# Gates of the recurrence on PSUM banks of their own, in regrouped blocks, with the engines' orders around them rewritten

## The reference

```
proj = h @ w_in[l]
xr, yr, q, k, v, g_a, g_b = jnp.split(proj, IN_SPLITS, axis=-1)
u  = causal_depthwise_conv(xr, conv_w[l], conv_b[l])        # width 4
r  = sigmoid(block_diag_linear(u, rg_w_a[l], rg_b_a[l]))    # 16 blocks of 88 x 88
i  = sigmoid(block_diag_linear(u, rg_w_x[l], rg_b_x[l]))
log_a = -8 * r * softplus(-lam);  a = exp(log_a)
inp = sqrt(-expm1(2 * log_a)) * (i * u)
hr = scan(h[t] = a[t] * h[t-1] + inp[t])
y_a = (gelu(yr) * hr) @ w_up_a[l]
```

## Time and profile before

| | |
|---|---|
| median of 3 runs | 2631.21 us (2628.38 to 2634.86) |
| profiled execution | 2633.96 us, span 2632.1 us |
| PE busy | 2610.1 us, 99% |
| POOL, ACT, DVE busy | 1127.0, 1116.0, 882.9 us |
| DMA | 263.01 MB, mean 100 GB/s |
| mean granted clock of TensorE | 0.997 |

### The profile page before, as it was taken

How to read it: one execution, slowest core, us unless ns; L and a number is a source line. 1 busy time by engine, 2 the same in 40 slices (tenths; PEclk the granted TensorE clock), 3 DMA queues, 4 the chain that set the end, 5 groups by cost and what they waited for, 6 DMA issues and landing times.

```text
span 2632.1 us, 31945 instructions
## 1 busy us (share of the span) xinstructions
PE 2610.1 (99%) x11808; PEld 2121.9 (81%) x11808; DVE 882.9 (34%) x1585; ACT 1116.0 (42%) x1635; POOL 1127.0 (43%) x478
## 2 busy tenths in 40 slices
PE   9999999999999999999999999999999999999999
PEld 7888887778877788888888888868788778888887
DVE  4223135661346332221132231447513453322210
ACT  5333245743546443332243332457435463433321
POOL 4444444355431344444444444444553314444443
PEclk9999999999999999999999999999999999999999
DMA  5333624323323223333333323343233232333322
GB/s 160 98 96 98 220 87 120 98 91 109 98 73 97 82 89 103 96 96 97 97 103 96 96 92 98 87 125 90 89 114 92 69 101 89 96 96 96 96 92 76
DMA packets 258134, 263.01 MB, mean 100 GB/s; under 512 B 9606, under 2 KB 242006, under 8 KB 258038
## 3 DMA queue, kind: packets, MB, share of 16 engines
q1 hardware_dynamic: 253542, 253.09, 32.3%
q10 hardware_dynamic: 4496, 8.58, 1.0%
HBM read 252.25 MB, written 10.57 MB: 100 GB/s over the span
## 4 chain that ended last, share of the span: by engine, by line
issue 47%; PE 30%; POOL 23%; POOLq 1%; DVE 0%
POOL wlo L551 23%; PE ps L1350 8%; PE ps L1355 8%; PE ps L1354 8%; PE ps L1563 1%; PE ps L1621 1%; PE ps L1636 1%; PE ps L1581 1%; PE ps L1586 1%; PE ps L1585 1%; POOLq L550 0%; POOLq L556 0%; PE ps L1543 0%; PE ps L1544 0%; PE ps L1413 0%
## 5 line engine op out<-in xcount | busy, mean ns | idle before, releaser
L551 POOL TENSOR_TENSOR wlo<-raw,whi 128x1024 fp32r<-128x1024 f32 x466 | 1125.7, 2418 | 1483.6 <-ACT whi L575 1483.5
L1350 PE MATMUL ps<-h_lo,whi 128*128 128x512 f32 x2272 | 890.0, 392 | 7.1 <-POOL wlo L551 6.2
L1354 PE MATMUL ps<-h_hi,whi 128*128 128x512 f32 x2272 | 887.0, 390 | 0.0
L1355 PE MATMUL ps<-h_hi,wlo 128*128 128x512 f32 x2272 | 886.6, 390 | 0.0
L575 ACT ACTIVATE whi<-raw 128x1024 fp32r<-128x1024 f32 x466 | 489.3, 1054 | 754.1 <-PE ps L1350 709.2
L1350 PEld LDWEIGHTS ps<-h_lo,whi 128*128 128x128 f32 x2272 | 428.3, 188 | 103.3 <-POOL wlo L551 7.9
L1355 PEld LDWEIGHTS ps<-h_hi,wlo 128*128 128x128 f32 x2272 | 428.1, 188 | 89.7
L1354 PEld LDWEIGHTS ps<-h_hi,whi 128*128 128x128 f32 x2272 | 428.3, 188 | 88.3
L1350 PE MATMUL ps<-act_lo,whi 128*128 128x512 f32 x704 | 274.1, 389 | 0.0
L1355 PE MATMUL ps<-act_hi,wlo 128*128 128x512 f32 x704 | 274.0, 389 | 0.0
L1354 PE MATMUL ps<-act_hi,whi 128*128 128x512 f32 x704 | 274.0, 389 | 0.0
(11 more groups left out here) (192 smaller groups left out, 2562.1 us busy)
## 6 DMA issues: line engine op xcount, KB each, us to landing
raw<-in_w_in SPq DMA_DIRECT2D x124, 512.0 KB
raw<-in_w_gate SPq DMA_DIRECT2D x88, 512.0 KB
raw<-in_w_up SPq DMA_DIRECT2D x88, 512.0 KB
raw<-in_w_down SPq DMA_DIRECT2D x80, 512.0 KB
rel_band<-rel_rows ACTq DMA_DIRECT2D x1, 8192.0 KB, 41.9
raw<-in_w_up_b SPq DMA_DIRECT2D x16, 512.0 KB
raw<-in_w_out SPq DMA_DIRECT2D x16, 512.0 KB
raw<-in_w_up_a SPq DMA_DIRECT2D x16, 384.0 KB
```

Source lines behind the costliest of these rows:

```text
L551: nc.gpsimd.tensor_tensor(wlo[:, s, :], raw[:, s, :], whi[:, s, :].bitcast(F32), ALU.subtract).then_inc(lo_made, 1)
L1350: ins = pe.matmul(ps[:, b, :], w_hi, x_lo, start=start, stop=False)
L1354: pe.matmul(ps[:, b, :], w_hi, x_hi, start=False, stop=False)
L1355: return pe.matmul(ps[:, b, :], w_lo, x_hi, start=False, stop=stop)
```

## The change

Gates get banks 6, 7, 0, 1 in turn, xr tiles 2 to 5; yr's banks are put in another order, the rest follows. Blocks are regrouped, the fifth group stands behind the first chunk of yr's first pair instead of behind the pair, and its order is 8, 14, 9, 15, 10. ACT does the sigmoids of a group ahead of the rounding of the next chunk; DVE does all of `u_gated` behind tile 10; the gelus are taken out of the loop that splits the product. SP's moves are put in between other loads.

```diff
--- before.py
+++ after.py
@@ -47,7 +47,7 @@
 
 NB = RNN // RB
 REST, MAIN = P - RB, KR
-GROUPS = [[0, 1], [2, 3, 11], [4, 5, 12], [6, 7, 13], [8, 9, 10, 14, 15]]
+GROUPS = [[0, 1], [2, 3], [4, 5, 11], [6, 7, 12, 13], [8, 14, 9, 15, 10]]
 GATED = [b for group in GROUPS for b in group]
 HELD = 4
 
@@ -334,17 +334,12 @@
         def mix_bank(n):
             return 2 + n % 6
 
-        def in_turn(*order):
-            bank, n = {}, 2
-            for kind, first, last in order:
-                for t in range(first, last):
-                    bank[kind, t] = mix_bank(n)
-                    n += 1
-            return bank
-
-        BANK = in_turn(("xr", 0, 6), ("gate", 0, 4), ("xr", 6, 8), ("gate", 4, 10), ("xr", 8, 10), ("gate", 10, 16),
-                       ("xr", 10, 11), ("gate", 16, 22), ("yr", 0, 2), ("gate", 22, 32), ("yr", 2, KR), ("g", 0, KD),
-                       ("ua", 0, KD), ("qk", 0, 2 * KD))
+        def laid(kind, *banks):
+            return {(kind, t): b for t, b in enumerate(banks)}
+
+        BANK = {**laid("xr", 2, 3, 4, 5, 2, 3, 4, 5, 2, 3, 4), **laid("gate", *[6, 7, 0, 1] * (NB // 2)),
+                **laid("yr", 5, 2, 7, 6, 3, 4, 5, 2, 7, 6, 3), **laid("g", 4, 5, 6, 7, 2, 3, 4, 5),
+                **laid("ua", 6, 7, 2, 3, 4, 5, 6, 7), **laid("qk", *[mix_bank(n) for n in range(2 * KD)])}
 
         V_BANKS = [4, 5, 2, 3, 6, 4, 5, 7]
         UB_T, OUT_T = 0, KD
@@ -454,29 +449,29 @@
                 pairs(w_in, KD, l, XR0 + 3 * PAIR, 1, G8)
                 gate_weights(1)
                 pairs(w_in, KD, l, XR0 + 4 * PAIR, 1, G8)
+                u_moves(l, 11)
                 gate_weights(2)
                 last_tile(XR0)
-                u_moves(l, 11)
                 gate_weights(3)
+                u_moves(l, 12)
                 half_pair(YR0, 0, 0)
-                u_moves(l, 12)
+                gate_weights(4)
                 half_pair(YR0, 0, 1)
-                gates_move(l, 11)
-                gate_weights(4)
                 u_moves(l, 13)
                 half_pair(YR0, 1, 0)
                 half_pair(YR0, 1, 1)
-                gates_move(l, 12)
+                gates_move(l, 11)
                 half_pair(YR0, 2, 0)
                 u_moves(l, 14)
                 half_pair(YR0, 2, 1)
+                u_moves(l, 15)
+                gates_move(l, 12)
                 gates_move(l, 13)
                 half_pair(YR0, 3, 0)
-                u_moves(l, 15)
+                gates_move(l, 14)
                 half_pair(YR0, 3, 1)
+                gates_move(l, 15)
                 half_pair(YR0, 4, 0)
-                gates_move(l, 14)
-                gates_move(l, 15)
                 half_pair(YR0, 4, 1)
                 last_tile(YR0)
                 pairs(w_in, KD, l, G0, KD // 2, G8)
@@ -754,30 +749,28 @@
                 act.wait_ge(decay_made, C.next(decay_made))
                 conv_init(6)
                 conv_init(7)
+                gates(2, 3)
                 ring()
-                gates(2, 3, 11)
                 conv_hi(6)
                 conv_hi(7)
                 ring(2)
                 conv_init(8)
                 conv_init(9)
+                gates(4, 5, 11)
                 ring()
-                gates(4, 5, 12)
                 conv_hi(8)
                 conv_hi(9)
-                ring(2)
+                ring()
                 conv_init(10)
                 gates(6, 7)
                 conv_hi(10)
-                gates(13)
+                gates(12, 13)
+                ring(2)
+                decayed(0, 2)
+                gates(8, 14, 9, 15, 10)
+                ring(2)
+                decayed(2, KR)
                 ring()
-                decayed(0, 2)
-                ring()
-                decayed(2, 4)
-                ring()
-                gates(8, 9, 10, 14, 15)
-                ring()
-                decayed(4, KR)
                 act.preload_act_table_set("natural_log_exp_and_others")
                 act.wait_ge(tanh_made, C.now(tanh_made))
                 for m in range(KR + 2):
@@ -796,19 +789,25 @@
 
 
 
-                ring()
-                for t in range(KR + 2):
-                    if t < KR:
+                def gelu(*tiles):
+                    for t in tiles:
                         b = BANK["yr", t]
                         C.step(bank_read[b])
                         act.wait_ge(bank_read[b], C.now(bank_read[b]))
                         nc.scalar.activation(y[:, t, :], y[:, t, :], ACT.Gelu_apprx_tanh
                                              ).then_inc(gelu_made, C.made(gelu_made))
-                    if t == KR:
+
+                ring()
+                gelu(0, 1, 2, 3)
+                ring()
+                gelu(4, 5, 6, 7)
+                ring()
+                gelu(8, 9, 10)
+                for t in range(KR):
+                    hi_of(ya_hi[:, t, :], tmp[:, t % 2, :])
+                    if t == 2:
                         act.preload_act_table_set("sigmoid_and_others")
-                    if t >= 2:
-                        hi_of(ya_hi[:, t - 2, :], tmp[:, t % 2, :])
-                    if t in (1, 3, 5, 7, 9, 11):
+                    if t in (1, 4, 7, 10):
                         ring()
 
                 for t in range(KD):
@@ -1129,6 +1128,7 @@
 
                 def u_gated(*tiles):
                     for t in tiles:
+                        dve.wait_ge(gate_made, gates_through(l, t))
                         for b in rest_of(t):
                             dve.wait_ge(gates_moved[(b - MAIN) % 2], moved(l, b, 2))
                         nc.vector.tensor_tensor(u[:, t, :], u[:, t, :], i_gate[:, t, :], ALU.mult
@@ -1139,12 +1139,10 @@
                 u_made(4, 5)
                 u_made(6, 7)
                 u_made(8, 9)
-                u_gated(0, 1)
                 u_made(10)
-                u_gated(2, 3)
+                u_gated(0, 1, 2, 3, 4, 5, 6, 7, 8, 9, 10)
                 yr_out(0)
                 yr_out(1)
-                u_gated(4, 5, 6, 7, 8, 9, 10)
 
                 for m in range(KR + 3):
                     if m in (3, 7, 11):
@@ -1485,8 +1483,8 @@
                 def xr(t, **how):
                     pair(G8, KD, (BANK["xr", t], BANK["xr", t + 1]), h_hi, h_lo, for_dve, t == 0, **how)
 
-                def yr(t):
-                    pair(G8, KD, (BANK["yr", t], BANK["yr", t + 1]), h_hi, h_lo, for_dve, False)
+                def yr(t, **how):
+                    pair(G8, KD, (BANK["yr", t], BANK["yr", t + 1]), h_hi, h_lo, for_dve, False, **how)
 
                 def gates(group):
                     s = chunk()
@@ -1521,8 +1519,7 @@
                 gates(GROUPS[2])
                 single(BANK["xr", KR - 1], h_hi, h_lo, for_dve)
                 gates(GROUPS[3])
-                yr(0)
-                gates(GROUPS[4])
+                yr(0, behind=lambda g: g == 0 and gates(GROUPS[4]))
                 yr(2)
                 yr(4)
                 yr(6)
@@ -1539,7 +1536,7 @@
                     for n in (t, t + 1):
                         C.step(square_made)
                         pe.wait_ge(square_split, C.next(square_split))
-                        pe.wait_ge(bank_read[n % 2], C.now(bank_read[n % 2]))
+                        bank_free(n % 2)
                         pe.matmul(ps[:, n % 2, :], ones_head[:, :], square_lo[:, n % 2, :], start=True, stop=False)
                         pe.matmul(ps[:, n % 2, :], ones_head[:, :], square_hi[:, n % 2, :], start=False, stop=True
                                   ).then_inc(square_used, C.made(square_used))
```

## The result

| | before | changed |
|---|---|---|
| median of 8 runs | 2632.69 us (2628.38 to 2635.36) | 2639.11 us (2637.64 to 2643.73) |
| profiled execution, span | 2633.96, 2632.1 us | 2641.95, 2640.2 us |
| mean granted clock | 0.997 | 0.993 |

The ratio is 1.003, 95% interval 1.0021 to 1.0039: slower by 6.4 us, or 8.1 us in the profiled executions. The forecast was 2616 us, 2603 to 2625; the kernel came out above that range.

The account below looks back on a forecast made before the run. The prediction took TensorE, busy 99% of the span, as the bound, with time lost only in late matmul starts. From 2631.2 us, -18.3 + 8.4 + 3.8 - 9.0 = -15.1 us gave 2616 us, range 2603 to 2625.

Parts of the forecast that it names:

- Most to gain: Late matmul starts from the first group's last gate to w_up_a, both layers: 27.6 us, 1.05% of the span.
- Banks: Gate groups up to yr: new banks remove PE's waits, 7.8 us in layer 0, 10.5 in layer 1, -18.3 us in total.
- with its own two turns of banks again 0.5 us in time: Gate group 4 (blocks 6, 7, 12, 13): its reused banks are free 0.5 us before PE needs them.
- Rival (b): New wait plus more: bank turns of groups 3 and 4 missed, or log phase not sooner; 2622 to 2628 us, 22%.
- New wait before block 15: Fifth gate group: PE waits for block 14's sigmoid, itself behind block 12's moves out; 4.2 us a layer, +8.4 us.
- The 2.0 us that the prediction quotes: Transfer setup and completion for the moves before block 15; with it the wait would be 3.3 us, the sum 1.8 better.
- The clock behind it: Matmuls after the wait before block 15 run at the low clock: 1.9 us each, +3.8 us, between 0 and 5.6.
- Later stretch: From yr to w_up_a: an earlier log phase and regrouped gelus remove PE's waits for wlo, -9.0 us.
- the moves are issued by 473.8 and landed at 476 to 477.3: Block 15's moves out, layer 0: so timed, they start the log phase near 481.6, 4.8 us sooner.
- Rival (c): Slower: block 12's moves land far later than 3.5 us after issue; at 12.5 us more per layer 2641 us; 4%.
- so no new wait: Before w_up_a: with the gelus out of it, the gated-product chain gets shorter, adding no wait.

Follow-up runs that it names:

- f2: f1 plus e4's edit (high halves of tiles 8 and 9 made ahead of the two roundings): 2607.49 us, ratio 0.9911.
- e4: Changed kernel, with ScalarE making the high halves of tiles 8 and 9 ahead of the two weight roundings, not between them: 2639.58 us, ratio 1.0026.
- f3: f2 with the gelus put back in the loop that splits the product: 2606.93 us, ratio 0.9903.
- e3: Changed kernel, with block 15's moves out put ahead of the load of chunk 23 on SyncE's list: 2630.03 us, ratio 0.999.
- e5: Kernel before, with the load of chunk 25 put ahead of block 15's moves out: 2638.72 us, ratio 1.0028.
- e2: Changed kernel, with g's banks reordered so that g tile 2 follows yr tile 7, not yr tile 9: 2632.86 us, ratio 1.0002.
- e1: Changed kernel, with block 12's moves out put ahead of the load of chunk 21 and block 15's input: 2631.48 us, ratio 0.9997.
- f1: Changed kernel, with the moves out of blocks 11, 12, 13, 15 and block 15's input each ahead of the load they stood behind: 2616.46 us, ratio 0.9942.
- e8: Changed kernel, with block 15's moves out put behind the load of chunk 24 as well as chunk 23: 2645.55 us, ratio 1.0047.
- e7: Changed kernel, with ScalarE again rounding the next chunk ahead of the sigmoids of groups 2 and 3: 2636.47 us, ratio 1.0016.

## Why the prediction was wrong, step by step

**Most to gain, 27.6 us: right.** f2 took 25.9 of it out of the two stretches.

**Banks, -18.3 us: the mechanism right, a margin wrong.** xr pair 6 and groups 2 and 3 start without a wait, and 39.97 us for the stage is what e4, f2 and f3 measured (40.06 forecast). It came to -11.9 us. The step that failed is "group 4 ..., with its own two turns of banks again 0.5 us in time": it took DVE's scaling of tile 10 as free to run, and left out that the sigmoids moved ahead push two roundings together (438.21 and 440.19), so that GpSimd subtracts twice without a break and DVE's splits last until just behind it. That cost 1.7 us of late start a layer, and 0.9 and 2.3 us of half-speed matmuls behind it within the stage. Rival (b) had named this, and the phase that isn't sooner, without a cause.

**New wait before block 15, +8.4 us: right in place and in chain, in size by luck.** It measured 3.7 + 4.6 = 8.3 us, but PE itself came some 3 us late to block 15, held by block 12's wait. e4 has the group stage that the forecast assumed (PE done with block 9 at 457.95, forecast 458.1), and there the same chain starts block 15 late by 7.2 and 7.4 us, 14.6 in all: block 13's sigmoid waits 1.8 us for block 11's moves, which the chain left out, and the moves took 2.9 us to issue instead of 2.3. The 2.0 us that the prediction quotes, beside its sum, from the page "DMA: Bandwidth & Descriptors" of the Trainium skill stand there for a transfer issued from GpSimd; these moves are issued from SyncE, and landed in 2.96 us.

**The clock behind it, +3.8 us: mechanism right, size wrong.** It is 17 to 19 matmuls, nearly all at 0.43 us, 3.8 and 3.4 us, 7.2 in all, beyond the 5.6 given as the top, which was twice the longest run seen behind waits of 1.2 to 2.5 us. Block 12's slow run adds another 1.7 us at the head of the later stretch.

**Later stretch, -9.0 us: wrong, and this decided the sign.** It came to +2.8, a miss of 11.8 us. Two steps failed. First, "the moves are issued by 473.8 and landed at 476 to 477.3". The load ahead of them waited until 474.55, since the rounding that it hangs on began at 471.01 and not at 466.8: block 14's sigmoid came at 464.16, and behind it ACT had to wait for PE's half-speed matmuls, 0.54, 0.59 and 0.60 us between the last sigmoids. The sum had priced that clock on PE alone. So the moves were issued by 477.36, 3.6 us late, and landed at 483.66, 6.3 us after their last issue (6.1 in layer 1), against 2.2 to 3.5 in the earlier trace rows, where no load stood right ahead of them. So the phase was 2.2 us later instead of 4.8 sooner. That the place does this is shown from both sides: e3 takes the load away and starts the phase 6.8 us sooner, e5 puts one load ahead in the kernel before and loses 6.8 us (ratio 1.0028). Rival (c) named a late landing behind a load, but for block 12's moves, which landed in 2.96 us; the late one was block 15's. Second, "so no new wait": g's banks were not costed. Tile 2 of g takes the bank of yr tile 9, read out behind the scans. That is 3.8 us a layer, with 8 and 6 slow matmuls behind; e2 shows that other banks remove it, e3 that an early phase removes it too.

**Why the parts don't add.** On the changed kernel, e1, e2 and e3 are worth 7.6, 6.3 and 9.1 us and e4 nothing; once f1 has put SP in order, e4 is worth 9.0, and on top of that e2's banks under 1. In e4 PE reaches block 15 3.3 us sooner, but the sigmoid that frees its bank comes when SP's list lets it, at 464.31 against 464.16, and all that was won is waited away there. Only with the moves early (f1) is it kept. The other way round, e2's edit has nothing left to remove once the phase is early.

**Open.** How landing goes with the loads around it. From end of issue to the gating: 3.5 us with a load right behind (before), 4.2 and 4.0 with one ahead (e5), 4.5 and 5.2 with two ahead (e8), 5.4 to 6.3 with one ahead and one right behind (both layers of the changed kernel, e1, e2, e4 and e7). Loads on both sides cost more than two on one, but that is no rule either: in f2 block 15's moves took 6.5 and 5.9 us (end of issue 462.79 and 1756.27, gating at 469.28 and 1762.15, DVE idle before both), where two loads stood ahead of block 14's moves and the next load was issued 2.2 us behind. In the changed kernel the DMA engines are busy for 0.81 of 476 to 478 us, and more just after, as this view by stretches shows (columns as above, with all engines ahead of the clock; the last share, over 1, is as the profile gives it):

```profile
474.00:476.00 2.00, 2.00 (x10) 1.68 (x9) 0.00 (x0) 2.00 (x5) 1.96 (x2) 1.00 0.16 19
476.00:478.00 2.00, 2.00 (x10) 1.65 (x10) 0.00 (x0) 0.68 (x2) 0.96 (x1) 1.00 0.81 278
478.00:480.00 2.00, 2.00 (x11) 1.65 (x10) 0.00 (x0) 0.00 (x0) 0.00 (x0) 1.00 0.85 136
480.00:482.00 2.00, 2.00 (x11) 1.65 (x10) 0.00 (x0) 0.00 (x0) 0.00 (x0) 1.00 1.09 132
```

The page "DMA: Bandwidth & Descriptors" of the Trainium skill (issuing engines are not separate DMA queues) says that DMAs started by ScalarE, SyncE or GpSimd all run on the same 16 engines and interleave; with two 512 KB loads in these 6 us the trace fits that, but no run here separated sharing from order. It also isn't settled why some waits of about 3 us (e4, and layer 0 of e7, at g tile 2) have no slow matmuls behind them, while waits of 3.8 us at the same tile had some 6 to 14 (changed kernel, e1, e7, e8).

## What to carry to other kernels

In a list that is worked through in order, a small move that someone waits for belongs ahead of a large load that itself has to wait. Here the load brought its own wait (in e3, without it, the moves were issued 6.7 us sooner), and re-placing the moves alone (f1) was worth 22.7 us. How long they then take to land is another matter: 6.5 us in f2 too. Where a wait is removed from one place of a chain, ask first what the last link is, and test edits in that order; e4 looked worthless until f1 was in. When a bank table is rewritten, write down for every tile whose bank it takes and when that is read out, including tiles whose own code didn't change.

## What the runs showed of the hardware

- DVE's splits with both inputs in SBUF took 5.29 us for two beside GpSimd's subtractions and 1.29 us without them, each ending about 0.55 us behind a subtraction.
- Three small SBUF-to-SBUF moves took 2.1 to 3.1 us to issue and landed 2.2 to 6.5 us after their last issue, with no rule found for the loads around them.
- Behind the waits of 3.5 and 4.5 us before block 15 PE ran 19 and 17 matmuls at the 1.2 GHz level or between the two, 3.8 and 3.4 us lost, so these waits cost about twice their length. Behind the waits of 3.8 us at g tile 2 it ran only 8 and 6, and behind three of 2.8 to 3.0 us (e4, e7) none.
